# An MLP whose up projections all run before its down products, in pairs by seven block products

## The reference, cut to what matters

```python
hm = rms_norm(x, norm_mlp)                                  # (1088, 1024)
x = x + jnp.square(jax.nn.relu(hm @ w_up)) @ w_down         # w_up 1024 x 4096, w_down 4096 x 1024
y = rms_norm(x, norm_final)
```

## Time and profile before

| | before |
|---|---|
| median of 3 runs | 2209.72 us (2208.33 to 2210.82) |
| span of the profiled execution | 2207.2 us |
| TensorE busy | 2188.0 us, 99% of the span |
| VectorE, ScalarE, GpSimd busy | 50%, 30%, 50% |
| granted TensorE clock, mean | 0.998 of full speed (2.4 GHz) |

### The profile page before, as it was taken

How to read it: one execution, slowest core, us unless ns; L and a number is a source line. 1 busy time by engine, 2 the same in 40 slices (tenths; PEclk the granted TensorE clock), 3 DMA queues, 4 the chain that set the end, 5 groups by cost and what they waited for, 6 DMA issues and landing times. The chain is left out here.

```text
span 2207.2 us, 33503 instructions
## 1 busy us (share of the span) xinstructions
PE 2188.0 (99%) x13547; PEld 2073.1 (94%) x13547; DVE 1112.9 (50%) x1749; ACT 658.2 (30%) x1158; POOL 1094.1 (50%) x1363
## 2 busy tenths in 40 slices
PE   8999999999999999999999999999999999999998
PEld 7999999999999999999999999889989889899897
DVE  8522221799764535534443566455364463553625
ACT  5444442333321111232222212133223232232332
POOL 4544444677343233222225564418475575754851
PEclk9999999999999999999999999999999999999999
DMA  5233332112121111222334555201211202102022
GB/s 180 95 99 100 107 104 69 49 49 69 53 89 51 48 42 52 58 60 80 90 121 141 174 186 169 97 16 43 77 30 49 70 8 77 58 20 77 20 67 81
DMA packets 172941, 172.31 MB, mean 78 GB/s; under 512 B 6722, under 2 KB 147334, under 8 KB 172779
## 3 DMA queue, kind: packets, MB, share of 16 engines
q1 hardware_dynamic: 169905, 159.87, 23.6%
q0 software_dynamic: 2304, 8.91, 1.1%
q10 hardware_dynamic: 578, 1.38, 0.2%
HBM read 135.62 MB, written 34.89 MB: 77 GB/s over the span
## 5 line engine op out<-in xcount | busy, mean ns | idle before, releaser
L967 PE MATMUL acc<-h_hi,w_hi 128*128 128x368 f32 (+2 forms) x2040 | 669.6, 328 | 0.5 <-issue 0.5
L969 PE MATMUL acc<-h_hi,w_lo 128*128 128x368 f32 (+2 forms) x2040 | 663.5, 325 | 0.0
L968 PE MATMUL acc<-h_lo,w_hi 128*128 128x368 f32 (+2 forms) x2040 | 662.8, 325 | 0.0
L1952 POOL TENSOR_TENSOR w_lo<-w_raw,w_hi 128x256 fp32r<-128x256 f32 x508 | 378.1, 774 | 470.1 <-ACT w_hi L1464 470.1
L967 PEld LDWEIGHTS acc<-h_hi,w_hi 128*128 128x128 f32 x2040 | 383.4, 188 | 5.5 <-issue 4.0
L968 PEld LDWEIGHTS acc<-h_lo,w_hi 128*128 128x128 f32 x2040 | 383.5, 188 | 0.2
L969 PEld LDWEIGHTS acc<-h_hi,w_lo 128*128 128x128 f32 x2040 | 383.3, 188 | 0.0
L1464 ACT ACTIVATE w_hi<-w_raw 128x1024 fp32r<-128x1024 f32 (+2 forms) x145 | 138.7, 957 | 358.9 <-PE acc L969 183.8
L2310 DVE TENSOR_TENSOR x<-pz,x 128x512 f32<-128x512 f32 x214 | 144.3, 688 | 90.9 <-PE pz L969 88.3
L1952 POOL TENSOR_TENSOR a_op<-a_raw,a_op 128x256 fp32r<-128x256 f32 x196 | 157.8, 843 | 24.6 <-DVE a_raw L2310 14.9
L2310 DVE TENSOR_TENSOR a_raw<-acc,a_raw 128x368 f32<-128x368 f32 (+1 forms) x112 | 44.8, 421 | 206.9 <-ACT a_raw L1827 118.7
(11 more groups left out here) (530 smaller groups left out, 4687.5 us busy)
## 6 DMA issues: line engine op xcount, KB each, us to landing
w_raw<-in_w_in SPq DMA_DIRECT2D x70, 512.0 KB, 4.3
w_raw<-in_w_up SPq DMA_DIRECT2D x32, 512.0 KB, 4.3
gate_values<-staging SPq DMA_DIRECT2D x29, 544.0 KB, 3.7
gsig<-gate_values SPq DMA_DIRECT2D x29, 544.0 KB, 3.7
w_raw<-in_w_down SPq DMA_DIRECT2D x18, 512.0 KB, 3.5
b_raw<-branch_outputs POOLq DMA_DIRECT2D x16, 544.0 KB, 5.5
w_raw<-in_w_branch SPq DMA_DIRECT2D x16, 512.0 KB, 4.8
g_raw<-in_w_in SPq DMA_DIRECT2D x14, 512.0 KB, 5.3
```

The lines of the kernel that those rows point to most:

```text
L967: pe.matmul(out, lh, rh, start=first, stop=False, skip_group_check=more)
L968: pe.matmul(out, lh, rl, start=False, stop=False, skip_group_check=more)
L969: return pe.matmul(out, ll, rh, start=False, stop=last, skip_group_check=more)
L1952: return pool.tensor_tensor(out, x, y, op)
```

## The change

Only the MLP and what its operands need of memory are changed. A round no longer holds an up and a down part.

1. The four units that came last (28 to 31) are computed first, by the old form (`last_up`). Their ReLU and square are both on ScalarE, and SP stores the result to DRAM (`last_store`).
2. During them VectorE and ScalarE make the sums `t_op` of the normed rows' blocks (`v_t_sums`, `v_t_high`), and SP stores the residual to DRAM (`x1_kept`), since its room in SBUF is now used for other things.
3. The other 28 units run in 14 pairs by seven block products (`up_pairs`), in the form and on the banks of `pairs`. VectorE adds, squares (ReLU and square in one instruction) and makes the sums that the down products need (`v_finish`), and SP stores them to DRAM (`v_store`).
4. Seven rounds of `down` follow one another. SP loads each stage's left operand (512 KB, `op_load`) into one of six places, up to six stages ahead; ScalarE makes its high part (`a_high`), and its low part is made by VectorE at stages 1, 3 and 5 (after the first two) and by GpSimd at the others (`a_low`).
5. The residual is loaded again around the end of the pairs (`x1_load`), partly over the second half of `h_hi` and `h_lo`. The values of the last four units are loaded and split in rounds 2 to 5 (`u_high`, `u_low`), and the 36 last groups use them as before.

TensorE's queue, and the parts of VectorE's queue that matter most:

```diff
-            for i in range(END):
-                for s in range(4):
-                    up(i, s)
-                down(i)
-            for s in range(4):
-                up(END, s)
+            for e in range(LAST):
+                last_up(e)
+            up_pairs()
+            for i in range(NR):
+                down(i)
...
+            def v_finish(j):
+
+                v_square(j, "12", "g_act", 8 * j + 8)
+                one, two = staging[:, 2 * (j % 2), :], staging[:, 2 * (j % 2) + 1, :]
+                if j:
+                    dve.wait_ge(*v_stored(j + 1))
+                dve.wait_ge(sem("v_squared"), 3 * LAST + 4 * j + 4)
+                tt(v_sums[:, 0, :], one[:, 512:TP], one[:, 0:512], ALU.subtract).then_inc(sem("v_summed"), 1)
+                tt(v_sums[:, 2, :], one[:, 512:TP], two[:, 512:TP], ALU.add).then_inc(sem("v_summed"), 1)
+                dve.tensor_copy(packs_raw[:, j % 2, 0:2, TS:], staging[:, 2 * (j % 2):2 * (j % 2) + 2, TP:]) \
+                    .then_inc(sem("v_summed"), 1)
+                tt(packs_raw[:, j % 2, 2, TS:], one[:, TP:], two[:, TP:], ALU.add).then_inc(sem("v_summed"), 1)
+                dve.wait_ge(sem("v_summed"), 6 * j + 1)
+                tt(v_sums[:, 1, :], v_sums[:, 0, :], two[:, 512:TP], ALU.add).then_inc(sem("v_summed"), 1)
+                dve.wait_ge(sem("v_summed"), 6 * j + 5)
+                tt(v_sums[:, 3, :], two[:, 0:512], v_sums[:, 1, :], ALU.subtract).then_inc(sem("v_summed"), 1)
...
+            def up_pairs():
+                for j in range(VP):
+                    if j:
+                        v_op_sums(j, (2,))
+                        v_finish(j - 1)
+                    v_add(j, 1, "11", 0)
+                    v_square(j, "11", "g_dve", 6 * j + 2)
+                    v_op_sums(j, (3,))
+                    if j + 1 < VP:
+                        v_op_sums(j + 1, (0, 1))
+                    v_add(j, 4, "22", 4)
+                    v_square(j, "22", "g_dve", 6 * j + 4)
+                    v_add(j, 5, "21", 2)
+                    v_square(j, "21", "g_dve", 6 * j + 6)
...
+            v_t_sums()
+            up_pairs()
+            down_sums(0, 1)
+            v_finish(VP - 1)
+            dve.wait_ge(sem("g_done"), V_DONE + 2 * OPS_V - 4)
+            link(dve.memset(x1_s[TS:], 0.0))
+            pack_low(0)
+            for i in range(NR):
                 for e, (st, p) in enumerate(DOWN):
                     down_add(i, e)
-                    if e + 1 == STAGE_END[0]:
-                        down_sums(i, 3)
-                    if e + 1 == STAGE_END[3]:
-                        down_sums(i, 6)
+                    n = 7 * i + st
+                    if e + 1 == STAGE_END[st]:
+                        if n + 2 in DVE_LO:
+                            a_low(n + 2)
+                        if st in (0, 3):
+                            down_sums(i, st + 3)
+                        elif st == 5 and i + 1 < NR:
+                            down_sums(i + 1, 1)
```

GpSimd's queue, and where `down` waits:

```diff
+            for n in range(OPS_V):
+                v_low(n)
+            b_low(0)
+            a_low(0)
+            a_low(1)
+            for n in range(1, OPS_D):
+                b_low(n)
+                if n + 1 < OPS_D:
+                    a_low(n + 1)
+                if n % 7 == 6 and 2 <= n // 7 < 6:
+                    u_low(n // 7 - 2)
...
                     if st != stage:
                         stage = st
-                        pe.wait_ge(sem("op_lo"), OPS_G + 7 * i + st + 1)
-                        pe.wait_ge(sem("u_ready"), 16 * i + A_READY[st])
+                        pe.wait_ge(sem("op_lo"), OPS_G + OPS_V + n + 1)
+                        pe.wait_ge(*a_low_ready(n))
...
                     if p == 4:
                         if st == 0:
-                            pe.wait_ge(sem("u_ready"), 16 * i + 11)
+                            pe.wait_ge(sem("packed"), i + 1)
```

More of the change, by code:

```diff
@@ L297 @@
 SAMPLES = {0: (0, 0), 1: (0, 1), 4: (2, 1), 5: (1, 0)}
-A_READY = (9, 11, 12, 13, 14, 15, 16)
-U_ORDER = ([0, 1, 2, 3, 4, 5, 6, 7], [0, 1, 7, 2, 3, 4, 5, 6])
+A_SLOTS = 6
+DVE_LO = [n for n in range(2, OPS_D) if n % 7 in (1, 3, 5)]
+POOL_LO = [n for n in range(OPS_D) if n not in DVE_LO]
 def down_bank(st, p):
@@ new lines, in _ @@
+            wide_hi(L_U + 1)
+            for e in range(LAST):
+                for g in range(3):
+                    last_square(e, g)
+                    if (e, g) in ((0, 2), (1, 0), (2, 0), (2, 1)):
+                        v_t_high(((0, 2), (1, 0), (2, 0), (2, 1)).index((e, g)))
+                    if g == 2 and e < 2:
+                        wide_hi(L_U + 2 + e)
+                    if (e, g) == (3, 0):
+                        v_high(0)
+                        v_high(1)
+            v_high(2)
@@ L2293, in _ @@
+            for e in range(1, LAST):
+                wide_lo(L_U + e)
+            for n in range(OPS_V):
+                v_low(n)
[6 more added lines that the diff above has]
+                    a_low(n + 1)
+                if n % 7 == 6 and 2 <= n // 7 < 6:
+                    u_low(n // 7 - 2)
+            e_low(0)
+            e_low(2)
             for n, c in enumerate(ORDER):
@@ new lines, in v_square, with v_add @@
+            def v_square(j, corner, ready, count):
+                dve.wait_ge(sem(ready), (V_DVE if ready == "g_dve" else V_ACT) + count)
+                v = v_value(j, corner)
+                stt(v, v, 0.0, v, ALU.max, ALU.mult).then_inc(sem("v_squared"), 1)
+            def v_add(j, e, corner, copied):
+                for c in range(2):
+                    dve.wait_ge(sem("g_done"), V_DONE + 14 * j + 2 * e + c + 1)
+                    dve.wait_ge(sem("g_act"), V_ACT + 8 * j + copied + c + 1)
+                    v = v_value(j, corner, c)
+                    tt(v, v_bank(j, e, c), v, ALU.add).then_inc(sem("g_dve"), 1)
@@ new lines, in pack_low, with up_pairs @@
+            def pack_low(i):
+                dve.wait_ge(sem("g_sig"), 3 * PAIRS + i + 1)
+                tt(packs_d[:, :, :, TS:], packs_in[:, :, :].rearrange("p q (s n) -> p q s n", s=3),
+                   packs_d[:, :, :, 0:TS].bitcast(F32), ALU.subtract).then_inc(sem("packed"), 1)
+            def up_pairs():
+                for j in range(VP):
+                    if j:
[10 more added lines that the diff above has]
+                    v_square(j, "21", "g_dve", 6 * j + 6)
@@ L3011, in down_add @@
                         dve.wait_ge(sem("l_added"), added[c, hh])
[L3012 removed]
+                    else:
+                        back(c, hh)
+                    ins = tt(tile(c, hh), bank, tile(c, hh), ALU.add)
                     added[c, hh] = 32 * i + e + 1
                 ins.then_inc(sem("l_added"), 1)
[L3016 to L3025 removed]
+            v_t_sums()
```

899 lines of the change are left out of this document (540 added, 359 removed).

## The result

The changed kernel takes 2193.4 us (median of 4 runs, 2190.6 to 2197.4), against 2209.8 us for the kernel before (median of 4): a ratio of 0.993 with a 95% interval of 0.991 to 0.994. It is faster by 16 us where 30 were forecast, and it lies just above the range. The profiled execution, the shortest of the four, spans 2188.8 us, 18.4 us less than before. One execution of the kernel before, of the seven taken beside the last four experiments, took 4363.3 us and is left out of every figure here.

What follows compares the result with a forecast made beforehand. TensorE, busy 99% of the span, was taken as the bound. Matmuls -37.3, first pair +1.1, junction +5 and rounds +1.5 gave -29.7 us: span 2177.5, median 2180 us, range 2172 to 2192.

Steps and rivals of the forecast that it cites:

- The matmuls: Up projection on TensorE: 14 pairs at 21.08 us each replace the old form's 23.75, a change of -37.3 us.
- the four odd units are only moved: The four up units now computed first: moving them was taken to change no time.
- First pair: Start of the 14 up pairs: fed like the first gate pair, 1.1 us of waiting, from 0 to 3.
- The sentence on ScalarE's copies of these sums: Odd units: the copies stand ahead of ReLUs, but each ends before TensorE returns to the bank, 8 us later.
- the sentence on product 3: First up pair: its operand is made behind the low parts of `t_op` and comes about as needed, at 56.6 us.
- The other pairs: Up pairs after the first: no cost, covered by the 3 to 9 us that VectorE idles in a pair.
- The rival in which VectorE is late: Up pairs: VectorE lags 1 us in each of 14 pairs, giving 2194 us; chance 0.04.
- Junction and rounds: From pairs to down rounds: 5 us (1 to 9) waiting for `pack_low`; all seven rounds: 1.5 us (-1.4 to 8).
- The rounds: Seven down rounds: GpSimd and VectorE both fit, rounds of 42.4 to 43.5 us, GpSimd 85 to 95% busy.
- the rival of a GpSimd bound: Down rounds: GpSimd's parts at 1.07 us each make it the bound, 2245 us; chance 0.08 in full form.
- that rival's partial form: Down rounds: GpSimd's parts cost a partial loss of 1 to 4 us a round, 2185 to 2206 us; chance 0.08.

Runs made afterwards that it cites:

- split4: Changed kernel with each 2176-column block sum and low part of `t_op` on VectorE cut into four instructions of 544 columns; 2186.2 us, ratio 0.990.
- tlow: Changed kernel with the four low parts of `t_op` one block sum earlier in VectorE's queue; 2188.5 us, ratio 0.990.
- pack: Changed kernel with the zero fill and first low part of `packs_d` ahead of the last pair's squares and sums on VectorE; 2194.4 us, ratio 0.993.
- dvelow: Changed kernel with the low parts of the second to fourth odd unit made by VectorE instead of GpSimd; 2182.9 us, ratio 0.988.
- psum: Changed kernel with the second operand of the nine block sums read from PSUM (values wrong, for times alone); 2184.5 us, single run.

## Why the prediction was wrong

**The matmuls: right, but for one clause.** Minus 37.3 us stands: 21.08 us a pair was forecast and measured. The step that failed is the half sentence that "the four odd units are only moved" and cost nothing. They cost 9.6 us. Moved, they lie beside VectorE's block sums, which I priced for VectorE alone, as the start of the first pair needs them; whose instructions run beside them, and on which ports, I did not ask. The mechanism itself was in the prediction, for the rounds: I gave GpSimd a slow rate of 1.07 us a part from rows taken beside instructions of 512 columns, where GpSimd and VectorE alternate. Beside 2176 columns the same rule gives 2.9. The row for it was there: `t_raw` at 2783 ns. The odd units' low parts, four for each unit, due 12 us apart, would have been the first thing to check. The kernel before even has a measured row: in its first gate pair two of GpSimd's low parts run beside the same block sums of 2176 columns and take 2.8 us each. GpSimd of the kernel before, 40 to 75 us:

```profile
50.92 5.55 POOL L1952 TENSOR_TENSOR w_lo<-g_raw,w_hi 128x256 fp32r<-128x256 f32 x2 [10.93 <-ACT w_hi L1464]
```

Four low parts at that price are 11 us. In the kernel before, the second unit's begin at 1484.3 and are needed at 1488.3, 4 us later, so this row gives an estimate of 7 us of waiting there.

**First pair: 3.3 us where 1.1 were taken,** just over my bound of 3. The block sums and the low parts of `t_op` came when the text said, within some 3 us beside the shift of the odd units. The sentence on ScalarE's copies of these sums held: in the odd units TensorE never waits for ScalarE. What failed is the sentence on product 3. Its operand was priced by its own due time alone, and its sum was indeed made near it, 8.2 us after the pair's start where product 3 was due at 9.1. But its high part stands in ScalarE's queue ahead of the copies of product 0's banks, which product 2 needs, and waits there for a sum behind VectorE's 10.5 us. That path had no term.

**The other pairs: right,** no wait in 13 of them. The rival in which VectorE is late did not come; that its time, 2194 us, is near the measured one is chance.

**Junction and rounds: 5 + 1.5 forecast, 6.2 measured,** place and name right, with `pack_low` 10.0 us after the last product (forecast 7 to 11). I had priced it as a wait for `pack_low`; neither of the two other orders tried mends it, since the sums that then come last are waited for in its place.

**The rounds: right.** After the first, at 48.1 us, they take 42.1 to 43.5 us each. GpSimd is busy 260 of 303 us, 86%; its parts there, 1878 to 2130 us:

```profile
L2200 POOL TENSOR_TENSOR a_op<-a_raw,a_op 128x256 fp32r<-128x256 f32 x92 | 77.0, 870 | 0.1
L2200 POOL TENSOR_TENSOR w_lo<-w_sum,w_hi 128x256 fp32r<-128x256 f32 x48 | 36.0, 782 | 24.3 <-ACT w_hi L1718 19.0 <-DVE f_raw L2544 5.2
...
L2200 POOL TENSOR_TENSOR w_lo<-w_raw,w_hi 128x256 fp32r<-128x256 f32 x32 | 22.6, 742 | 0.0
```

All parts of 256 columns in this stretch take 0.80 us on average, under the 0.99 us from which the rival of a GpSimd bound would have decided. The time that rival's partial form named (2185 to 2206) came true by another road, in the odd units. The sum as it came: -37.3 + 3.3 + 6.2 = -27.8 (28.0 by the stretches), and + 9.6 for the odd units. The span is 11.3 us above the forecast of 2177.5. The median is 13.4 above its 2180: it lies 4.6 us above the changed kernel's profiled span, where 2.5 were taken, since that profile was the shortest run.

## What to carry to other kernels

When work is moved, price what it does to its new neighbours, not only whether it is itself in time: list the other engines' instructions in the stretch that it moves to. A GpSimd instruction on SBUF beside a run of VectorE instructions with two SBUF operands takes at least the length of one of those, so long block sums don't go beside low parts that TensorE waits for. Give such parts to VectorE, place the sums where GpSimd is idle, or keep one operand in PSUM (tried here for its time alone). And in a queue served in order, look at what an instruction that waits for late data has behind it: the two best edits here changed no work, only who does it and when.

## What the runs showed of the hardware

- The hold lasts for the whole VectorE instruction and works both ways: 0.71 us became 2.9 for GpSimd, and 2.42 became 2.83 to 2.96 for VectorE's 2176 columns. I had expected a fixed slow rate.
- VectorE's pieces back to back can keep GpSimd out past the end of one instruction: single parts of 256 columns took 7.0 and 6.7 us beside pieces of 544 columns in split4, while others beside the same pieces took 1.2.
- A wait costs more than its length. After the 7.7 us gap TensorE issued 13 matmuls at 1.2 GHz (2.0 us), after the gap of 4.6 us in the first round 6 of them in the changed kernel (1.4 us) and 13 in tlow (2.8 us). After the gap of 3.3 us in the first pair none did in the changed kernel, nor in pack. In dvelow the granted clock behind it was 0.50 from 1533.0 to 1535.8 us, and the pairs took 299.95 us, 1.5 more; psum and split4 show the same. The same edit can look 1 to 3 us better or worse in one profile for that reason.
